# Prompt attention: three banks instead of two for turned probabilities, one instead of two for values, and the scalar engine's exponentials moved ahead of its copies

## The reference, cut to what matters

```python
def nsa_attend_block(q, gates, qpos, kc, vc, ks_blk, vs_blk, kw, vw, wpos):   # 128 queries a time
    p_c = masked_softmax(einsum('bqghd,bngd->bghqn', qg, kc) * scale, mask_c)  # 32 compressed keys
    o_c = einsum('bghqn,bngd->bqghd', p_c, vc)
    ...   # choice of blocks: with 16 blocks in all and TOP_N = 16, every block is chosen
    p_s = masked_softmax(einsum('bqghd,bgqkd->bghqk', qg, kg) * scale, mask_s) # all keys up to the query
    o_s = einsum('bghqk,bgqkd->bqghd', p_s, vg)
    p_w = masked_softmax(einsum('bqghd,blgd->bghql', qg, kw) * scale, mask_w)  # the last 512 keys
    o_w = einsum('bghql,blgd->bqghd', p_w, vw)
    o = g[:, :, 0] * o_c + g[:, :, 1] * o_s + g[:, :, 2] * o_w
```

## Time and profile before

| what | value |
|---|---|
| time, three runs | 1835.75, 1838.21, 1843.84 us; median 1838.21 us |
| profiled execution | 1841.63 us, of which the span that the trace covers 1839.7 us |
| instructions | 26664 |
| PE busy, share of the span | 1645.3 us, 89% |
| stage of the prompt attention | 358 to 665 us of the span |
| PE, DVE, ACT busy in that stage | 277.2, 182.1, 152.5 us of 307 us |

### The profile page before, as it was taken

One profiled execution on the slowest core, in us unless ns is written; L12 is line 12 of the kernel. 1 busy time (PEld: TensorE's weight loads), 2 busy tenths in 40 slices (PEclk: granted clock), 3 DMA queues, 4 the chain that ended last, 5 costly groups with the idle time before them and its releaser, 6 DMA issues. The chain is left out here.

```text
span 1839.7 us, 26664 instructions
## 1 busy us (share of the span) xinstructions
PE 1645.3 (89%) x11237; PEld 1252.3 (68%) x11237; DVE 761.2 (41%) x1276; ACT 582.4 (32%) x1111; POOL 360.3 (20%) x230
## 2 busy tenths in 40 slices
PE   4899798699888879999999958898999989997598
PEld 4345466466656559999988747785999965553375
DVE  2221111265666556660088744233321434444343
ACT  4001111155544453222146533333431302222221
POOL 1111000011000012231189734110220200000131
PEclk8999898799999999999999989998999999998699
DMA  9222263232111001111101164112100120002621
GB/s 330 78 79 46 69 158 81 70 107 93 47 47 47 2 6 46 47 46 46 27 26 33 46 170 155 57 50 73 37 24 24 46 92 1 24 24 92 220 92 63
DMA packets 120572, 129.88 MB, mean 71 GB/s; under 512 B 16728, under 2 KB 92938, under 8 KB 120326
## 3 DMA queue, kind: packets, MB, share of 16 engines
q1 hardware_dynamic: 120102, 128.08, 22.2%
q0 software_dynamic: 352, 0.10, 0.2%
HBM read 107.05 MB, written 23.18 MB: 71 GB/s over the span
## 5 line engine op out<-in xcount | busy, mean ns | idle before, releaser
L154 PE MATMUL banks<-h_T_high,w_ssd_high 128*128 128x352 f32 x480 | 155.8, 325 | 0.7 <-ACT h_T_high L1418 0.7
L154 PE MATMUL banks<-h_T_rest,w_ssd_high 128*128 128x352 f32 x480 | 156.0, 325 | 0.0
L154 PE MATMUL banks<-h_T_high,w_ssd_rest 128*128 128x352 f32 x480 | 155.2, 323 | 0.0
L154 PE MATMUL banks<-w_attn,h_T 128*128 128x408 f32 (+5 forms) x432 | 148.6, 548 | 0.0
L154 PEld LDWEIGHTS banks<-w_attn,h_T 128*128 128x128 f32 (+1 forms) x432 | 74.3, 183 | 73.2 <-issue 56.0
L154 PE MATMUL banks<-w_r,h_T 128*128 128x512 f32 (+1 forms) x320 | 118.0, 556 | 0.0
L1249 DVE TENSOR_REDUCE neg_max_att<-banks 128x1 f32<-128x512 f32 (+7 forms) x128 | 84.3, 668 | 45.3 <-PE banks L154 44.7
L154 PE MATMUL banks<-out_even_w_high,mix_high 128*128 128x512 f32 (+1 forms) x216 | 87.8, 407 | 16.4 <-DVE out_even_w_rest L2171 12.5
L1093 PE MATMUL banks<-const_f,p_att 128*128 128x128 f32 x512 | 80.1, 286 | 17.9 <-ACT p_T_att L1178 9.2
L1172 ACT ACTIVATE p_att<-banks,neg_max_att 128x512 f32<-128x512 f32 (+7 forms) x128 | 86.5, 677 | 26.1 <-DVE neg_max_att L1249 24.5
L1093 PEld LDWEIGHTS banks<-const_f,p_att 128*128 128x128 f32 x512 | 54.2, 141 | 54.2 <-ACT p_T_att L1178 14.9
(11 more groups left out here) (482 smaller groups left out, 3462.8 us busy)
## 6 DMA issues: line engine op xcount, KB each, us to landing
w_mod_late<-in_w_mod_dram SPq DMA_DIRECT2D x8, 2048.0 KB, 8.1
w_ssd<-in_w_in_even_dram SPq DMA_DIRECT2D x20, 512.0 KB, 3.9
w_mod_rows<-in_w_mod_dram SPq DMA_DIRECT2D x4, 2048.0 KB, 21.2
xin<-in_x_prompt_dram SPq DMA_DIRECT2D x8, 512.0 KB, 6.3
cmp_w<-in_nsa_cmp_w_dram SPq DMA_DIRECT2D x8, 512.0 KB
silu_z_T<-in_state_ssd_dram SPq DMA_DIRECT2D x8, 512.0 KB, 4.2
out_dram<-silu_z_T SPq DMA_DIRECT2D x8, 512.0 KB, 3.6
out_even_x_rows<-in_x_prompt_dram SPq DMA_DIRECT2D x8, 512.0 KB, 3.6
```

The lines of the kernel that those rows point to most:

```text
L154: return nc.tensor.matmul(out, lhsT, rhs, start=start, stop=stop, skip_group_check=True)
```

## The change

Group g of turned data goes to bank 4 + g % 3 (banks 4, 5, 6) and waits for the copy of group g - 3. All values go to bank 7, and the first values of a branch (hh 0) wait until `scale` of the branch just before is done (`o_scaled` at q, where before it was q - 1). In ACT's order each `head_exp` of unit n+1 comes ahead of the copy of unit n that it stood behind. The order of PE and of DVE is unchanged, apart from which bank and which count they use. The coefficients, the samples and the late modulation rows share the rotating banks and follow the same rule.

```diff
         def wait_copied(eng, g):
-            eng.wait_ge((copied_dve, copied_act)[engine_of[g]], order_of[g])
+            if g >= 0:
+                eng.wait_ge((copied_dve, copied_act)[engine_of[g]], order_of[g])
...
                     for g, s, blocks in some:
-                        if g >= 2:
-                            wait_copied(pe, g - 2)
+                        if g >= 3:
+                            wait_copied(pe, g - 3)
                         for x, (b, half) in enumerate(blocks):
...
-                            last = nc.tensor.transpose(e.ps[:, 4 + g % 2, x * P:(x + 1) * P], src, e.ident)
+                            last = nc.tensor.transpose(e.ps[:, 4 + g % 3, x * P:(x + 1) * P], src, e.ident)
...
-                    bank = 6 + q % 2
-                    if q >= 2 and hh == 0:
-                        pe.wait_ge(o_scaled, q - 1)
+                    bank = 7
+                    if q and hh == 0:
+                        pe.wait_ge(o_scaled, q)
...
                     for x in range(max(len(mine), len(heads))):
+                        if x < len(heads):
+                            head_exp(n + 1, heads[x])
                         if x < len(mine):
                             copy_group(mine[x])
-                        if x < len(heads):
-                            head_exp(n + 1, heads[x])
```

More of the change, by code:

```diff
@@ L1034, in mod_job @@
                     pe.wait_ge(wm_in, 16 * (j + 1))
-                    wait_copied(pe, g - 2)
-                    mod_products(nc, e, wm, 4 + g % 2).then_inc(t_done, 1)
+                    wait_copied(pe, g - 3)
+                    mod_products(nc, e, wm, 4 + g % 3).then_inc(t_done, 1)
                     if j in (3, 5):
                         wait_copied(pe, g)
-                        wait_copied(pe, g - 1)
-                        mod_turn(nc, e, mrow, 4 + (g + 1) % 2, 0).then_inc(t_done, 1)
+                        wait_copied(pe, g - 2)
+                        mod_turn(nc, e, mrow, 4 + (g + 1) % 3, 0).then_inc(t_done, 1)
                 def old_scores(n):
@@ L1099, in turn_coef @@
                     pe.wait_ge(coef_ready, 3 * i + kind + 1)
-                    wait_copied(pe, g - 2)
+                    wait_copied(pe, g - 3)
                     for hh in range(HG):
-                        last = nc.tensor.transpose(e.ps[:, 4 + g % 2, hh * P:(hh + 1) * P], scaled[:, i % 2, kind, hh * P:(hh + 1) * P], e.ident)
+                        last = nc.tensor.transpose(e.ps[:, 4 + g % 3, hh * P:(hh + 1) * P], scaled[:, i % 2, kind, hh * P:(hh + 1) * P], e.ident)
                     last.then_inc(t_done, 1)
@@ L1138, in turn_samples @@
                     pe.wait_ge(o_smp_in, 16 * G)
-                    wait_copied(pe, g - 2)
+                    wait_copied(pe, g - 3)
                     for hh in range(HG):
-                        last = nc.tensor.transpose(e.ps[:, 4 + g % 2, hh * TS:(hh + 1) * TS], A.o_smp[:, hh * P:(hh + 1) * P], e.ident[0:TS, 0:TS])
+                        last = nc.tensor.transpose(e.ps[:, 4 + g % 3, hh * TS:(hh + 1) * TS], A.o_smp[:, hh * P:(hh + 1) * P], e.ident[0:TS, 0:TS])
                     last.then_inc(t_done, 1)
@@ L1177, in copy_group @@
                     act.wait_ge(t_done, g + 1)
-                    nc.scalar.copy(pT[:, s, 0:len(blocks) * P], e.ps[:, 4 + g % 2, 0:len(blocks) * P]).then_inc(copied_act, 1)
+                    nc.scalar.copy(pT[:, s, 0:len(blocks) * P], e.ps[:, 4 + g % 3, 0:len(blocks) * P]).then_inc(copied_act, 1)
                 def copy_coef(i, kind):
@@ L1185, in copy_coef @@
                         act.wait_ge(o_scaled, q - 1)
-                    nc.scalar.copy(coefT[:, q % 2, :], e.ps[:, 4 + g % 2, :]).then_inc(copied_act, 1)
+                    nc.scalar.copy(coefT[:, q % 2, :], e.ps[:, 4 + g % 3, :]).then_inc(copied_act, 1)
                 for n in range(-1, len(units)):
@@ L1203, in _ @@
                             act.wait_ge(gates_saved, 16 * 8)
-                        nc.scalar.copy(mrow[:, j % 2, :], e.ps[:, 4 + g % 2, 0:P]).then_inc(copied_act, 1)
+                        nc.scalar.copy(mrow[:, j % 2, :], e.ps[:, 4 + g % 3, 0:P]).then_inc(copied_act, 1)
             @block.gpsimd
@@ L1255, in copy_group @@
                         part = lambda x: pT[:, s, x * G * P:(x + 1) * G * P].rearrange("p (g t) -> p g t", g=G)
-                        src = e.ps[:, 4 + g % 2, 0:G * P].rearrange("p (g t) -> p g t", g=G)
+                        src = e.ps[:, 4 + g % 3, 0:G * P].rearrange("p (g t) -> p g t", g=G)
                         link(nc.vector.tensor_tensor(part(0), src, e.F["tri"][:, None, :].broadcast_to([P, G, P]), ALU.mult))
@@ L1259, in copy_group @@
                         return
-                    nc.vector.tensor_copy(pT[:, s, 0:len(blocks) * P], e.ps[:, 4 + g % 2, 0:len(blocks) * P]).then_inc(copied_dve, 1)
+                    nc.vector.tensor_copy(pT[:, s, 0:len(blocks) * P], e.ps[:, 4 + g % 3, 0:len(blocks) * P]).then_inc(copied_dve, 1)
                 def close(n):
@@ L1284, in scale @@
                     wait_copied(dve, closing[i, kind])
-                    nc.vector.tensor_tensor(scaled[:, i % 2, kind, :], e.ps[:, 6 + q % 2, :], coefT[:, q % 2, :], ALU.mult).then_inc(o_scaled, 1)
+                    nc.vector.tensor_tensor(scaled[:, i % 2, kind, :], e.ps[:, 7, :], coefT[:, q % 2, :], ALU.mult).then_inc(o_scaled, 1)
                 for n in range(-1, len(units)):
@@ L1305, in _ @@
                         z = A.oT[:, :, TP:T]
-                        nc.vector.tensor_tensor(z, e.ps[:, 4 + sample_group % 2, 0:HG * TS].rearrange("p (h t) -> p h t", h=HG), z, ALU.mult).then_inc(copied_dve, 1)
+                        nc.vector.tensor_tensor(z, e.ps[:, 4 + sample_group % 3, 0:HG * TS].rearrange("p (h t) -> p h t", h=HG), z, ALU.mult).then_inc(copied_dve, 1)
                     if n in jobs and jobs[n] in (3, 5):
@@ L1309, in _ @@
                         dve.wait_ge(t_done, g + 1)
-                        mod_finish(nc, e, link, 1, jobs[n] // 2 - 1, 4 + g % 2, 0)
+                        mod_finish(nc, e, link, 1, jobs[n] // 2 - 1, 4 + g % 3, 0)
                         dve.sem_inc(copied_dve, 1)
```

2 lines of the change are left out of this document (1 added, 1 removed).

## The result

| | before | changed |
|---|---|---|
| median of 6 runs | 1836.35 us (1833.71 to 1843.84) | 1825.36 us (1823.13 to 1832.31) |
| profiled execution | 1841.63 us | 1830.52 us |
| its span, granted clock | 1839.7 us, 0.95 | 1828.6 us, 0.948 |
| the stage, first compressed scores to last `scale` | 304.13 us | 294.52 us |

The ratio of the times is 0.9943, 95% interval 0.9918 to 0.9968: 0.6% faster. Of the 11.08 us between the spans of the two profiled executions 9.61 lie in the stage that the diff touches.

What follows compares the result with a forecast made beforehand. PE, busy 89% of the span, was taken as the bound, so only its waits could be won. 9.5 + 1.8 + 0.1 - 0.3 - 1.4 = 9.7 us less gave 1829 us from 1838.2; range 1820 to 1837.

Steps and rivals of the forecast that it cites:

- Joined units, 9.5 gained: Sixteen joined rounds: third bank ends the third group's 0.69 us copy wait; 0.65 us each in fifteen, 9.5 us gained.
- Wide units, 1.8 gained: Sixteen wide rounds: 4.1 and 1.3 us gained, 3.6 lost, together 1.8 us gained.
- five "issue" rounds: Wide rounds where PE goes on by itself after the copy waits; those waits shrink, 4.1 us gained.
- four with ACT's copy first: Four-group units: ACT's first copy, now behind the next exponential, delays the fourth group; 3.6 us lost.
- The 1.3 us of four other wide rounds: Rounds whose next scores wait for p_ready: ACT's second copy no longer precedes the exponential; 0.15 to 0.5 us each.
- Narrow units, 0.1 gained by ACT's order: Units up to i 3, no bank waits: five gains of 0.1 to 0.5 us, three losses of 0.2 to 0.4.
- Compressed unit of i 4, 0.3 lost: Its round: the copy of 256 columns comes before the exponential that the scores wait for; 0.3 us lost.
- One bank for values, 1.4 lost: A branch's first values wait for the previous branch's scale, in six places in i 0 to 2; 1.4 us lost.
- That all copy waits go: Rival: each group finds a free bank and nothing new appears; 24.1 us gained, 1814 us; chance 0.06.
- That there would be no gain: Rival: in wide and joined units the maximum and exponential chain ends last; under 3 us, 1837; chance 0.12.
- The slower rival: ACT's first copy behind the next exponential holds the bank in every wide unit; 1846.5 us; chance 0.05.
- The falling clock: Rival: PE's clock falls in the new pauses, three or four falls costing 6 us; 1834.5 us; chance 0.15.

Runs made afterwards that it cites:

- The run with the short copy last: On the changed kernel, ACT does the first copy, both exponentials of the next unit, then the other copies; 1820.09 us, ratio 0.9913.
- the kernel with two bank plans: First copy, both exponentials, other copies, plus two banks for turned data and two for values until i 4, then three and one; 1816.07 us, ratio 0.9896.
- the one with DVE's first copies: On the changed kernel, DVE copies the first and third group of four-group units, ACT the second and fourth; 1827.67 us, ratio 0.9925.

## Why the prediction was right, and which of its steps were not

The forecast was 9.7 us less in the stage; it was 9.61. The time of 1829.0 was taken from the median shown then; from the later one of 1836.35 it would be 1826.7, and 1825.36 was measured. The interval of the ratio lies on both sides of the 0.5% line, as the forecast did.

- **Joined units, 9.5 gained.** Right: 9.83 profiled. Fifteen rounds gave 0.58 to 0.69. The term was slightly small because the round was put at 3.36 us, set by the later exponential; it is 3.32, set by PE. The run with the short copy last shows that the exponential has room.
- **Wide units, 1.8 gained.** 2.03. The five "issue" rounds gave 3.99 of 4.1, the four with ACT's copy first lost 3.32 of 3.6, +1.11 and +1.12 as forecast, +0.35 for 0.4, and in (6, hh 0) +0.74 for 1.0.
- **The 1.3 us of four other wide rounds** came as 1.36, but the reason given was wrong. It was put down to ACT's second copy no longer standing ahead of the exponential. With the old order the same rounds gain 0.15, 0.32, 0.31 and 0.41, 1.19 together: it is the third bank, and the order adds 0.17. In three of them it lets the last group be turned sooner, so that ACT's second copy is sooner out of the way: the second exponential starts 2.86 us after the round's first transposes and not 3.04 in (6, hh 1) and (6, hh 2), 3.18 and not 3.60 in (7, hh 0). In (5, hh 1) both exponentials start where they did, after 1.61 and 2.57 us, and it was PE that was late. These are its first scores of the next unit, in the kernel before and with three banks and the old order:

```profile
527.75 0.11 PEld L154 LDWEIGHTS banks<-const_bf 128*128 128x128 bf16 x2 [0.17 <-ACT p_att L1172]
```

```profile
522.67 0.11 PEld L154 LDWEIGHTS banks<-const_bf 128*128 128x128 bf16 x2 [0.87 <-ACT p_att L1173]
```

  The 0.17 us before them is the gap that PE shows between two kinds of work also where it is named "issue", as ahead of the values in the earlier trace rows. The prediction took it for a wait for `p_ready`; PE was held up by 0.87 us for a copy instead, and with the third bank it waits 0.87 us for the exponential.
- **Narrow units, 0.1 gained by ACT's order.** Wrong in sign: 0.95 lost, 2.00 less the 1.05 of the single bank. The prediction counted five gains and three losses, in i 0 and 1, and took i 2 and 3 for none. Against the old order there are three gains of 0.1 to 0.2 us, as in (0, br 0, hh 3), 1.61 to 1.38, and six losses of 0.1 to 0.4, the largest (1, br 0, hh 1), 2.25 to 2.67, three of them in i 2 and 3, as (3, br 0, hh 1), 3.35 to 3.63. One such round of the changed kernel:

```profile
385.75 0.47 ACT L1173 ACTIVATE p_att<-banks,neg_max_att 128x256 f32<-128x256 f32 x1 [1.16 <-DVE neg_max_att L1250]
386.21 0.57 ACT L1179 COPY p_T_att<-banks 128x512 f32<-128x512 f32 x1
...
386.68 0.48 ACT L1173 ACTIVATE p_att<-banks,neg_max_att 128x256 f32<-128x256 f32 x1
...
387.31 0.42 PEld L1094 LDWEIGHTS banks<-const_f,p_att 128*128 128x128 f32 x4 [0.76 <-ACT p_att L1173]
```

  ACT idled 1.16 us for the maximum with the copy behind it, then did the copy between the two exponentials, and PE's next transposes wait for the second.
- **Compressed unit of i 4, 0.3 lost.** 0.27.
- **One bank for values, 1.4 lost.** 1.05, by the run with that edit alone. Where the earlier trace rows had no wait there is now this one:

```profile
371.54 0.69 DVE L1286 TENSOR_TENSOR o_scaled<-banks,coef_T 128x512 f32<-128x512 f32 x1 [1.08 <-ACT coef_T L1187]
...
372.29 0.20 PEld L154 LDWEIGHTS banks<-p_T_att,kv_rows 128*64 128x64 f32 x4 [0.86 <-DVE o_scaled L1286]
```

The misses cancel: +0.3 joined, +0.2 wide, -1.05 narrow, +0.35 for the bank. 9.83 + 2.03 - 0.95 - 0.27 - 1.05 = 9.6. The two large terms, the joined rounds and the four losing wide ones, were right by their mechanism; that the sum fits to 0.1 us is luck.

**The rivals.** That all copy waits go, and 24.1 us with them, is refuted: 15.2 us of them went, four grew. With the old order ACT's are all gone and 2.6 us of DVE's are left, and still the gain is 15.2 us and not 24.1, because in ten of the sixteen wide rounds PE then waits 0.3 to 1.2 us for the exponential before the next scores, which is what the prediction held against this rival, with nine places. The Trainium skill's rule of rotating independent groups through banks (Perfetto Trace Analysis, Optimizing Tensor Performance (Matmuls)) agrees with the trace in kind: the third bank alone is worth 16.3 us. That there would be no gain is refuted by the joined rounds. The slower rival's mechanism exists, in four rounds here and in most wide and all but the last of the joined ones with two banks (1.0211 by the order alone), but with three banks it needs four groups in a unit, as was held against it. The falling clock is in the last section: it did not fall behind the new pauses of the changed kernel's one profile, but nothing in the record shows that it could not.

What the prediction saw and did not draw out: by its own terms the order was a loss, 1.5 us in the joined rounds (11 with the bank alone, 9.5 with both), 3.6 - 1.3 in the wide ones and 0.3 in the compressed one, less 0.1, or 4.0 us. It never set that sum against the change as a whole. Measured it is 0.3, 4.1, 0.3 and, in the narrow rounds, 0.95: 5.6 us, a loss in every kind of round.

## What to carry to other kernels

How long a buffer is held is set by where its read-out stands in its engine's queue, not by how long the read-out takes: a copy of 0.57 us ahead of a wait of 2.60 is free, and behind it holds PE for 1.82; so put first on an engine what is ready first, above all ahead of an instruction that will wait. When a change has two parts, price each alone: here one was worth 15.2 us and the other took 5.6 back.

## What was not expected of the hardware

**The same pause is followed by a fall of the clock or not.** Before the last compressed unit's scores PE waits for an exponential. The same wait in the changed kernel and in the one with ACT's old order:

```profile
600.29 0.37 PE L154 MATMUL banks<-const_bf 128*128 128x128 bf16 x2 [1.83 <-ACT p_att L1173]
```

```profile
601.35 0.28 PE L154 MATMUL banks<-const_bf 128*128 128x128 bf16 x2 [1.83 <-ACT p_att L1173]
```

After the first the two matmuls already take 0.37 us and the round 7.88; after the second 0.28 and 6.23. Of eight profiles the clock fell behind this pause in three. It cost 1.67 us before and 1.65 in the changed kernel, 1.32 in the third. The new pauses of the changed kernel before a fourth group, 1.58 us twice, 1.34 and 0.87 us, were followed by none (stretch, length, engines' busy us, granted clock, DMA):

```profile
612.00:614.50 2.50, 0.92 (x9) 0.65 (x10) 1.77 (x3) 2.45 (x4) 0.00 (x0) 1.00 0.00 0
...
614.50:618.30 3.80, 3.80 (x42) 2.30 (x38) 0.57 (x1) 0.86 (x3) 0.00 (x0) 1.00 0.02 4
```

In the kernel with ACT's new order alone PE pauses for 1.74 or 1.75 us in eight joined rounds. The clock fell behind two of these pauses; this is one:

```profile
506.07 0.44 PE L1093 MATMUL banks<-const_f,p_att 128*128 128x128 f32 x2 [1.75 <-ACT p_T_att L1178]
```

```profile
504.50:506.40 1.90, 0.33 (x2) 0.20 (x2) 0.82 (x2) 1.64 (x4) 0.00 (x0) 1.00 0.00 0
506.40:509.90 3.50, 3.50 (x33) 2.94 (x32) 0.85 (x2) 0.56 (x3) 0.00 (x0) 0.51 0.00 0
```

From 506.4 on PE ran at 0.51, that is at 1.2 GHz, and the round took 6.97 us, where one of the same kind without a fall took 5.45: 1.5 us. (The wait at 615.76, shown above, is a pause of 1.74 us of the matmuls, without a fall.) In the same profile the clock also fell behind a pause of 1.78 us and behind both of 2.02, and twice close behind one of only 1.10 us, in (5, br 1, hh 3) and here in (6, br 1, hh 3):

```profile
625.87 0.69 PE L1093 MATMUL banks<-const_f,p_att 128*128 128x128 f32 x2 [1.10 <-ACT p_T_att L1178]
```

```profile
625.90:629.60 3.70, 3.70 (x46) 3.01 (x50) 1.65 (x4) 0.19 (x1) 0.00 (x0) 0.54 0.00 0
```

The third pause of 1.10 us, in (4, br 1, hh 3), brought none. So the length of a pause does not settle by itself whether a fall follows, and the prediction's worry about pauses just under the 1.83 of the earlier trace rows was not groundless: that 1.58 us brought no fall in its two places does not make such a pause safe. What decides between equal pauses stays open; no run tried it.

**Stages with the same instructions differ by up to 9 us between executions, in part with such falls.** Outside the stage the eight profiles took 1527.4 us (granted clock of the whole 0.955, the kernel with two bank plans) to 1536.2 us (0.948, the one with DVE's first copies). In the first the clock stood at 1.2 GHz for 154 us outside the stage, in the second for 177; but it did for 177 us in the changed kernel too, which took 1534.1, so the two don't go together exactly. The stretch from 200 to 300 us, ahead of the stage, gives an example, first the kernel before and then the changed one:

```profile
200.00:300.00 100.00, 85.52 (x484) 63.44 (x484) 12.44 (x36) 15.04 (x39) 2.33 (x5) 0.88 0.47 126
```

```profile
200.00:300.00 100.00, 86.25 (x516) 64.63 (x514) 12.44 (x36) 15.08 (x40) 2.33 (x5) 0.91 0.47 126
```

At 0.91 and not 0.88 the same 100 us hold 32 more matmuls, and the stage starts 3.9 us earlier, though not all of that comes from this stretch. An edit worth under 9 us is therefore better read from its own stage in the profile than from the medians.
